# A hybrid decoder layer with 32 experts on one core: the first expert's rows by matrix products, the router in four column groups, two row stores on SyncE and the third gather moved

## The chip, the cores and the metric

One core of a Trainium2 chip runs one layer of a decoder on 512 positions, in float32. The metric is the device time of one launch in microseconds (us). A core has five engines with an instruction queue each: TensorE (PE, its weight loads shown as PEld), VectorE (DVE), ScalarE (ACT), GpSimd (POOL) and SyncE (SP). Engines wait for each other through semaphores, and 16 DMA engines move data for all queues.

## What is computed

```python
h = rmsnorm(x, g_mix); p = h @ w_in                   # q, k, v | B, C, conv input
mix = concat(rmsnorm(attention(q, k, v), g_attn_out), rmsnorm(conv, g_conv_out))
x = x + mix @ w_out
h = rmsnorm(x, g_ffn)
logits = h @ w_router + b_router                      # 32 experts
top_val, top_idx = top_k(logits, 4); gates = softmax(top_val)
# each of the 512 tokens goes to its 4 experts:
act = clamped_swiglu(rows @ w1[e] + b1[e])            # 1024 -> 2 x 1024
y = act @ w2[e] + b2[e]                               # 1024 -> 1024
x = x + sum over the 4 experts of gate * y
out = rmsnorm(x, g_final)
```

## The kernel before

**Stages.** The first 150 us compute the projections, attention and convolution. The out-projection follows in four tiles of 128 tokens (TB = 4) and two halves of the contraction. VectorE adds each tile to the residual X (residual(t, n), line 1219), ScalarE squares and sums the rows, and VectorE writes the normed rows h2 (second_norm, 1229). ScalarE's queue stores them to DRAM as h2_rows (store_h2, 1681). TensorE transposes X (turn_h2), two engines copy the transposes to xnT (turned_h2), and router(t) (782) multiplies them with the router weights in eight full products, tokens on the partitions. VectorE's select(t) (1245) picks the four best experts of each token, rank(t) (798) counts tokens per expert by a product with a triangular matrix, and place (1267) builds 0/1 matrices pick (token by slot) for experts 0 and 1 of the run.

**Rows of an expert.** An expert of the first three in order has up to 96 rows (MANY). For these a product of pick with token numbers gives the list of tokens (tok_static), POOL fetches the rows from h2_rows by an indirect DMA (fetch, 1901), TensorE transposes them (turn_lines) and ScalarE copies the result to rowsT (turned_rows, 1709). For the later experts, POOL scatters each token's entry into a list in DRAM (16 indirect DMAs, line 1929) and reads the list back into slots (six DMAs, 1937 and 1939); VectorE turns entries to token numbers (list_tokens, 1442) and POOL scales them.

**Order of the experts.** The experts 0 and 1 come first; the others are sorted by their number of rows. VectorE does the sort (1319 to 1336), TensorE three small products with its result (866 to 868) and two for the overflow table (871, 872). VectorE waits for the latter (prefix_done, 1343) ahead of pick_third and list_entries. SyncE waits for order_ready before it loads the third expert's weights.

**The expert loop.** Per expert TensorE does, by compute(i, parity) (991): first_product(i) (w1, 8 chunks of the contraction), transposes of the next expert's rows (turn_block(i + 1)), second_product(i - 1) (w2), and transposes of this expert's activations (turn_act_of(i)). The order of each engine is written out by hand, and every engine runs its instructions in that order. VectorE does clamped, product and activated for each expert (elementwise, 1447); list_tokens stands between the first expert's and the second's. POOL's move(i) (1949) scatters results, fetches rows of expert i + 2 and copies a bias selection (select, 1858) that first_product(i + 1) waits for. Weights come through a ring of 20 slots of 1 MB; a load takes two slots, and SyncE issues it when TensorE has used the old content of both (slot_used). Expert 0 fills slots 0 to 7, expert 1 slots 8 to 15, and w2 of expert 0 slots 16 to 19. The third expert's w1 goes to slots 0 to 7, w2 of the second to 8 to 11, the fourth expert's w1 to 12 to 19, and w2 of the third expert to 0 to 3 again. 18 experts are of the big kind (96 rows), 14 of the small one (64 rows).

Of the kernel before, what the change touches and what calls it, by code (L numbers as in the profile page):

```python
# [5 lines left out]
F32 = mybir.dt.float32  # L6
# [56 lines left out]
PICKED = 3  # L63
OVF_W = 4
# [18 lines left out]
def layer_kernel(nc, x, g_mix, w_in, conv_w, sinks, g_attn_out, g_conv_out, w_out,  # L83
                 g_ffn, w_router, b_router, w1, b1, w2, b2, g_final, out):
    ctx = ExitStack()
    with ctx:
# [65 lines left out]
        ones_col = sb("ones_col", [P, 1])  # L152
        upto = sb("upto", [E, E], BF16)
# [7 lines left out]
        gain_col = sb("gain_col", [P, KT])  # L161
        conv_wc = sb("conv_wc", [P, CONV_K, CT])
# [69 lines left out]
        w_out_hi = ring1_r[:, KT // 2 * SLOT:].rearrange("p (c j n) -> p c j n", c=KT, j=2)  # L232
        cur_token = slots[:, LIST_BLOCKS, 0:2, 0:1]
# [83 lines left out]
        h2_turned, h2_stored, tokens_ready = sem("h2_turned"), sem("h2_stored"), sem("tokens_ready")  # L317
        h2T_a, h2T_b = sem("h2T_a"), sem("h2T_b")
        logits_done, wrt_ready, negtop_ready, gexp_ready = sem("logits_done"), sem("wrt_ready"), sem("negtop_ready"), sem("gexp_ready")
        chosen_ready, rank_done, entries_ready = sem("chosen_ready"), sem("rank_done"), sem("entries_ready")  # L320
        pick_ready, tok_summed, sort_ready, order_done, order_ready = sem("pick_ready"), sem("tok_summed"), sem("sort_ready"), sem("order_done"), sem("order_ready")
# [52 lines left out]
        def fetches(upto):  # L374

            return 16 * sum(2 if BIG[i] and i >= STATIC else 1 for i in range(upto + 1))
# [28 lines left out]
        def _(sp):  # L405
            with nc.allow_non_contiguous_dma(reason="small parameter columns"):
# [24 lines left out]
                sp.dma_start(gain_col[:, :], g_ffn[0].rearrange("(k p) -> p k", p=P)).then_inc(small_in, 16)  # L431

# [119 lines left out]
        def _(pe):  # L552
# [224 lines left out]
            def keep_busy(count):  # L777

                for _ in range(count):
                    mm(ps[:, 3, :], ones_bf[:, :], ones_bf[:, 0:1].to_broadcast([P, 512]), start=True, stop=True)  # L780

            def router(t):

                pe.wait_ge(h2T_a, t + 1)
                pe.wait_ge(h2T_b, t + 1)
# [6 lines left out]
                logits = ps[:, LOGIT_BANKS[t % 2], 0:E]  # L792
                for k in range(KT):
                    ins = mm(logits, xnT[:, k, t * P:(t + 1) * P], w_rt[:, k, :],
                             start=(k == 0), stop=(k == KT - 1))
                ins.then_inc(logits_done, 1)

            def rank(t):
# [4 lines left out]
                if t == 2:  # L803
                    pe.wait_ge(pick_ready, 2 * t)
# [43 lines left out]
            rank(3)  # L848
            keep_busy(5)

            pe.wait_ge(pick_ready, 2 * TB)
            for e in range(2):
                for t in range(TB):
                    for part in range(2):
                        ins = mm(ps[:, 5, e:e + 1], pick[:, e, t, :], tok_value[:, t, part:part + 1],
                                 start=(t == 0 and part == 0), stop=(t == TB - 1 and part == 1))
            ins.then_inc(tok_summed, 1)

            mm(ps[0:E, 4, 0:1], chosen_cum[:, TB, :], ones_bf[:, 0:1], start=True, stop=True)
            mm(ps[0:E, 4, E:2 * E], ones_bf[:, 0:E], chosen_cum[:, TB, :], start=True, stop=True).then_inc(counts_done, 1)  # L860
# [3 lines left out]
            keep_busy(14)  # L864
            pe.wait_ge(sort_ready, 1)
            mm(ps[0:1, 5, 2 * E:3 * E], expert_no[:, :], in_place[:, :], start=True, stop=True)
            mm(ps[0:3 * E, 5, 3 * E:4 * E], ident_bf[:, :, :].rearrange("e s f -> e (s f)"), in_place[:, :], start=True, stop=True)
            mm(ps[:, 5, 4 * E:6 * E], ones_bf[0:E, :], diag[:, :, :].rearrange("e s f -> e (s f)"), start=True, stop=True).then_inc(order_done, 1)
            keep_busy(8)
            pe.wait_ge(nb_ready, 1)  # L870
            mm(ps[0:OVF_ROWS, 4, 6 * E:7 * E], ovf_nb16[:, :], upto[:, :], start=True, stop=True)
            mm(ps[0:OVF_ROWS, 4, 7 * E:8 * E], ovf_nb16[:, :], ident_bf[:, 0, :], start=True, stop=True).then_inc(prefix_done, 1)
# [44 lines left out]
            def w1_product(big, parity, slot, x_of, amid=None):  # L917

                for k0 in range(0, KT, GROUP):
                    if k0 and amid:  # L920
                        amid()
                    for k in range(k0, k0 + GROUP):
                        r, done, value = slot(k)
# [67 lines left out]
            def compute(i, parity):  # L991
# [3 lines left out]
                if i:  # L995
# [4 lines left out]
                    second_product(i - 1, 1 - parity, B_Y)  # L1000
                    turn_act_of(i)

            keep_busy(8)
            turn_block(0)
            expert_blocks(compute)
            pe.wait_ge(lin_ready, E)
# [1013 lines left out]
```

## Time and profile before

| | us |
|---|---|
| median of 3 runs | 1217.02 (1215.52 to 1218.39) |
| the profiled execution, its own time | 1214.39 |
| its span | 1212.7 |
| PE busy in the span | 1162.1 (96%) |
| DVE, ACT, POOL busy | 308.2, 190.7, 179.8 |

The page's 40 slices show the DMA engines at 9 tenths or more from the seventh slice on, at about 425 GB/s in most, and PE at 9 almost all the way. The largest groups of instructions are the experts' products (L927, L934, L953, L959). PE's durations are modelled and overlap, so two engines can both look full: the waits, and the time that a load takes to land, tell which one holds the other. Line numbers are those of the kernel before; "<-" behind a row names what ended the idle time before it.

### The profile page before, as it was taken

The page shows a single profiled execution, that of the slowest core. Times are in us where ns is not written, and L with a number is a line of the kernel's source. Part 1 is how long each engine was busy: PE and PEld are TensorE (multiplying, and loading weights), DVE is VectorE, ACT ScalarE, POOL GpSimd, SP SyncE. Part 2 cuts the span into 40 slices and gives each one's busy share as a digit, 9 for nine tenths or more (in the row PEclk, how much of TensorE's full clock was granted, in tenths as well). Part 3 has the DMA queues.
Part 4 walks back from the last instruction along what each step waited for, and adds up shares of the span by engine and source line. Part 5 has one row for each costly group of instructions (what it writes and reads, how often), then busy time and mean ns, then how long its engine had stood idle before and what let it go on. Part 6 is the DMA issues. An engine that isn't in the chain of part 4 may idle for free. (4 is left out here: it accounts for less than half of the span.)

```text
span 1212.7 us, 16574 instructions
## 1 busy us (share of the span) xinstructions
PE 1162.1 (96%) x7102; PEld 480.4 (40%) x7102; DVE 308.2 (25%) x492; ACT 190.7 (16%) x378; POOL 179.8 (15%) x251
## 2 busy tenths in 40 slices
PE   8999999999999999999999999999999999999980
PEld 5777786333333333333333333333333333333330
DVE  6588667421111111111111111111111111111117
ACT  5443612100110100001100000110000011000002
POOL 5300000521211111110111111111111101111000
PEclk9999999999999999999999999999999999999995
DMA  9602665999999999999999999999999999999996
GB/s 326 218 1 70 234 269 198 318 379 426 424 428 425 427 424 426 425 426 427 427 425 423 428 427 425 426 426 428 425 426 427 425 425 425 428 424 427 425 374 252
DMA packets 52236, 454.40 MB, mean 375 GB/s; under 512 B 13108, under 2 KB 14404, under 8 KB 27488
## 3 DMA queue, kind: packets, MB, share of 16 engines
q1 hardware_dynamic: 43760, 433.90, 86.4%
q0 software_dynamic: 7664, 17.05, 3.7%
q10 hardware_dynamic: 736, 2.36, 0.5%
q8 instruction: 58, 0.95, 0.3%
q14 instruction: 18, 0.15, 0.0%
HBM read 442.73 MB, written 15.12 MB: 378 GB/s over the span
## 5 line engine op out<-in xcount | busy, mean ns | idle before, releaser
L927 PE MATMUL ps<-ring_a,blockT 128*64 128x512 f32 x1088 | 240.6, 594 | 4.6 <-DMA ring_a<-in_w 4.6
L1416 DVE TENSOR_SCALAR glu_c<-ps 128x768 f32<-128x768 f32 (+1 forms) x32 | 26.9, 842 | 786.1 <-PE ps L934 498.0
L927 PEld LDWEIGHTS ps<-ring_a,blockT 128*64 128x64 f32 x1088 | 75.3, 137 | 159.2 <-issue 146.2
L953 PE MATMUL ps<-ring_a,actT 128*64 128x512 f32 x608 | 136.7, 596 | 0.0
L1895 POOL DMA_INDIRECT scores<-h_rows,slots x29 | 30.7, 1059 | 487.5 <-PE ps L885 486.6
L1705 ACT ACTIVATE blockT<-ps 128x512 f32<-128x512 f32 x29 | 17.3, 597 | 542.9 <-PE ps L885 542.9
L927 PE MATMUL ps<-ring_b,blockT 128*64 128x512 f32 x384 | 85.1, 594 | 2.9 <-DMA ring_b<-in_w 2.9
L1911 POOL DMA_INDIRECT expert_rows<-normed,slots x32 | 33.4, 1043 | 270.1 <-ACT normed L1734 269.8
L934 PE MATMUL ps<-ring_a,blockT 128*32 128x512 f32 x608 | 72.4, 615 | 0.0
L953 PEld LDWEIGHTS ps<-ring_a,actT 128*64 128x64 f32 x608 | 41.6, 136 | 76.2 <-issue 74.3
L927 PEld LDWEIGHTS ps<-ring_b,blockT 128*64 128x64 f32 x384 | 26.6, 137 | 57.6 <-issue 52.1
L1438 DVE TENSOR_TENSOR glu_c<-lin_c,sig 128x512 f32<-128x512 f32 (+1 forms) x50 | 43.2, 921 | 3.4 <-ACT sig L1728 2.8
L927 PE MATMUL ps<-ring_c,blockT 128*64 128x512 f32 x192 | 43.5, 595 | 0.0
L927 PE MATMUL ps<-ring_d,blockT 128*64 128x512 f32 x192 | 43.2, 592 | 0.0
L953 PE MATMUL ps<-ring_b,actT 128*64 128x512 f32 x192 | 43.0, 595 | 0.0
L959 PE MATMUL ps<-ring_a,actT 128*32 128x256 f32 x704 | 42.5, 382 | 0.0
L600 PE MATMUL ps<-xnT_hi,ring_r 128*128 128x512 f32 x144 | 36.7, 397 | 1.4 <-DVE xnT_lo L1061 1.3
L934 PEld LDWEIGHTS ps<-ring_a,blockT 128*32 128x32 f32 x608 | 17.3, 108 | 52.4 <-issue 52.4
L596 PE MATMUL ps<-xnT_hi,ring_r 128*128 128x512 f32 x144 | 35.8, 391 | 1.7 <-DVE ring_r L1054 1.7
L927 PE MATMUL ps<-ring_a,rowsT 128*64 128x512 f32 x160 | 35.2, 594 | 1.0 <-ACT rowsT L1714 1.0
L1733 ACT ACTIVATE normed<-ps,slots 128x256 f32<-128x256 f32 x18 | 8.5, 474 | 173.0 <-PE ps L959 173.0
L589 PE MATMUL ps<-xnT_lo,ring_r 128*128 128x512 f32 x144 | 35.6, 389 | 0.0
(328 smaller groups left out, 1254.9 us busy)
## 6 DMA issues: line engine op xcount, KB each, us to landing
ring_a<-in_w SPq DMA_DIRECT2D x116, 2048.0 KB, 32.2
ring_b<-in_w SPq DMA_DIRECT2D x38, 2048.0 KB, 31.0
ring_d<-in_w SPq DMA_DIRECT2D x19, 2048.0 KB, 34.6
ring_c<-in_w SPq DMA_DIRECT2D x19, 2048.0 KB
ring_a<-expert_rows SPq DMA_DIRECT2D x16, 512.0 KB, 18.4
ring<-in_w_in SPq DMA_DIRECT2D x8, 768.0 KB, 20.7
X<-in_x SPq DMA_DIRECT2D x8, 512.0 KB, 6.4
ring<-in_w_out SPq DMA_DIRECT2D x8, 512.0 KB, 5.0
```

Source lines behind the costliest of these rows:

```text
L589: ins = mm(ps[:, bank, :], high[:, k, :], xnT_lo[:, :, k, :], start=False, stop=(last and k == KT - 1))
L596: ins = mm(ps[:, bank, :], low[:, k, :], xnT_hi[:, k, :], start=False, stop=(last and k == KT - 1))
L600: mm(ps[:, bank, :], high[:, k, :], xnT_hi[:, k, :], start=(k == 0), stop=False)
L927: ins = mm(ps[half * HALF:(half + 1) * HALF, b, :], x_of(k)[0], ring(r)[:, 0, at + half * 512:at + (half + 1) * 512], start=False, stop=(k ...
L934: mm(ps[q * QUARTER:(q + 1) * QUARTER, B_BOTH, :], x_of(k)[1], quarter_cols(w, q), start=False, stop=(k == KT - 1), tile_position=(0, q * ...
L953: ins = mm(ps[half * HALF:(half + 1) * HALF, bank, :], actT[:, s % 2 * W2_K + j, s // 2 * HALF:(s // 2 + 1) * HALF], ring(r)[:, 0, j * D + ...
L959: ins = mm(ps[q * QUARTER:(q + 1) * QUARTER, bank + 1, 0:256], actT[:, 4 + j, s * QUARTER:(s + 1) * QUARTER], ring(slot(s)[0])[:, 0, j * D ...
L1416: v.tensor_scalar(width(glu_c, big), width(ps_glu, big), LIMIT, None, ALU.min).then_inc(glu_ready, 1)
L1438: ins = v.tensor_tensor(turned.rearrange("p (k q) -> p q k", k=n), a_in.rearrange("p (q k) -> p q k", k=n), b_in.rearrange("p (q k) -> p q ...
L1705: a.activation(out[:, 0:4, :], ps[:, B_T, :].rearrange("p (c t) -> p c t", c=4), ACT.Copy).then_inc(done, 1 if big else 2)
L1895: g.indirect_dma_start(gathered[:, 0:512], None, h2_halves, bass.IndirectOffsetOnAxis(lists[:, HALVES, 0:1], 0), bounds_check=last_half_to ...
L1911: g.indirect_dma_start(y_halves, bass.IndirectOffsetOnAxis(slots[:, HALVES, i, 0:1], 0), gated_y[:, parity, 0:512], None, bounds_check=las ...
```

## The change

Expert 0's rows no longer come by a gather. After place, VectorE writes for each tile of tokens a float32 matrix first_pick(t) (128 tokens by 96 slots) that holds the row's 1/rms where token and slot match; TensorE multiplies the residual X with it (pick_rows, 8 chunks for each of 4 tiles), and ScalarE copies the sums to rowsT with the norm's gain as its scale (gain_chunk, a further small load at the start). The router has the weights as stationary operand, 32 columns, and two rounds of four chunks in four column groups; ScalarE copies the partial logits, and one product with stacked identities adds them up (logits). second_norm for the tiles 2 and 3 comes after the selections, and SyncE stores these rows. SyncE's load of slot 12 no longer waits for the first gather. The third expert's gather (fetch(2)) stands ahead of the 16 list scatters in POOL's order. The small products for sort, overflow table and third list stand inside expert 0's first product (before chunks 2, 4 and 6). VectorE's selections, copies and places are in another order.

```diff
@@ SyncE
-            load_first(4, 10)
-            sp.wait_ge(rows_in, fetches(0))
-            load_first(12)
+            load_first(4, 10, 12)
             sp.wait_ge(logits_done, TB)
             load_w2(0, 0, w2_slot(0, 0))
+            for t in range(2, TB):
+                sp.wait_ge(h2_ready, 2 * (t + 1))
+                sp.dma_start(h2_tiles[t, :, :], normed[:, t % 2, :]).then_inc(h2_late, 16)
             for i in range(2, E):
                 load(i, i % 2)
@@ TensorE
             def router(t):
                 pe.wait_ge(h2T_a, t + 1)
-                pe.wait_ge(h2T_b, t + 1)
...
                 for k in range(KT):
-                    ins = mm(logits, xnT[:, k, t * P:(t + 1) * P], w_rt[:, k, :],
-                             start=(k == 0), stop=(k == KT - 1))
-                ins.then_inc(logits_done, 1)
+                    g = k % 4
+                    if k == 4:
+                        pe.wait_ge(h2T_b, t + 1)
+                    ins = mm(ps[g * E:(g + 1) * E, bank, PARTS_AT:PARTS_AT + P], w_rt[:, k, :], xnT[:, k, t * P:(t + 1) * P],
+                             start=(k < 4), stop=(k >= 4), tile_position=(0, g * E))
+                ins.then_inc(parts_done, 1)
+
+            def logits(t):
+                pe.wait_ge(parts_ready, t + 1)
+                mm(ps[:, LOGIT_BANKS[t % 2], 0:E], logit_parts, stacked[:, :], start=True, stop=True).then_inc(logits_done, 1)
...
-            out_proj(3, 1, lambda: router(1))
+            out_proj(3, 1, lambda: (logits(0), router(1)))
             turn_h2(2)
+            logits(1)
+            keep_busy(3)
+            turn_h2(3)
             rank(0)
+            keep_busy(2)
+            def pick_rows(t, chunks=range(KT)):
+                pe.wait_ge(first_pick_ready, t + 1)
+                for k in chunks:
+                    by_chunk = X[:, t, :].rearrange("p (s q j) -> p s j q", j=2, q=P)
+                    ins = mm(ps[:, PICK_BANKS[k // 4], k % 4 * MANY:(k % 4 + 1) * MANY], by_chunk[:, k // 2, k % 2, :], first_pick(t),
+                             start=(t == 0 and k % 4 == 0), stop=(t == TB - 1 and k % 4 == 3))
+                return ins
+            router(2)
             rank(1)
-            turn_h2(3)
-            router(2)
             router(3)
-            pe.wait_ge(biases_ready, 2)
-            pe.wait_ge(cur_ready, 2)
-            keep_busy(4)
+            logits(2)
+            pick_rows(0)
+            logits(3)
+            pick_rows(1, range(4))
             rank(2)
-            keep_busy(8)
+            pick_rows(1, range(4, KT))
+            keep_busy(1)
+            pick_rows(2, range(4))
             rank(3)
-            keep_busy(5)
...
+            pick_rows(2, range(4, KT))
+            pick_rows(3).then_inc(rows_turned, 1)
...
+                if i == 0:
+                    amid = {2: order_sums, GROUP: overflow_sums, GROUP + 2: third_sums}
...
-            keep_busy(8)
-            turn_block(0)
             expert_blocks(compute)
@@ VectorE
             def place(first, end):
...
                 for t in range(first, end):
-                    for e in range(2):
-                        v.tensor_scalar(pick[:, e, t, :], iota_r[:, :], own_rank[:, t, e:e + 1], None, ALU.is_equal).then_inc(pick_ready, 1)
+                    v.tensor_scalar(first_pick(t), iota_r[:, 0:MANY], own_rank[:, t, 0:1], stat[:, H_R + t:H_R + t + 1],
+                                    ALU.is_equal, ALU.mult).then_inc(first_pick_ready, 1)
...
-            second_norm(2)
+            norm_scale(2)
             select(0)
-            select(1)
             residual(3, 1)
             turned_h2(2)
+            select(1)
+            turned_h2(3)
+            norm_scale(3)
             place(0, 2)
-            turned_h2(3)
+            select(2)
+            select(3, lambda: place(2, 3))
+            place(3, 4)
+            second_picks(0, TB)
+            second_norm(2)
             second_norm(3)
-            select(2)
-            select(3)
-            place(2, 4)
@@ ScalarE
+                if isinstance(i, int) and i == 0:
+                    for k in range(KT):
+                        ins = a.activation(rowsT[:, k, :], ps[:, PICK_BANKS[k // 4], k % 4 * MANY:(k % 4 + 1) * MANY], ACT.Copy,
+                                           scale=gain_chunk[:, k:k + 1])
+                        if k % 4 == 3:
+                            ins.then_inc(rows_ready, 1)
@@ POOL
-            pool.wait_ge(h2_stored, 16 * TB)
+            pool.wait_ge(h2_stored, 16 * 2)
+            pool.wait_ge(h2_late, 16 * 2)
             pool.wait_ge(rows_cleared, 1)
             pool.wait_ge(tok_ready, 1)
-            fetch(0)
-            pool.wait_ge(rows_turned, 1)
             fetch(1)
+            pool.wait_ge(tok_ready, 2)
+            pool.wait_ge(rows_turned, 2)
+            fetch(2)
             pool.wait_ge(list_written, 16)
             pool.wait_ge(entries_ready, TB + 1)
             for t in range(TB):
...
                     g.indirect_dma_start(list_dram, bass.IndirectOffsetOnAxis(row_i[:, t, k:k + 1], 0), entry[:, t, k, :], None,
-            pool.wait_ge(tok_ready, 2)
-            pool.wait_ge(rows_turned, 2)
-            fetch(2)
             pool.wait_ge(list_written, 16 * (1 + TB * TOPK))
```

## Rows read from the trace of the kernel before

**Rows 1.** Two stretches: us, busy us by engine, granted TensorE clock, DMA share, GB/s

```profile
core 0: us, PE busy (x) PEld busy (x) DVE busy (x) ACT busy (x) POOL busy (x), PEclk, DMA share, GB/s
280.00:920.00 640.00, 640.00 (x4038) 216.48 (x4038) 81.87 (x123) 62.04 (x119) 87.27 (x90) 1.00 1.01 426
920.00:1180.00 260.00, 250.83 (x1574) 84.73 (x1568) 34.46 (x46) 25.93 (x49) 32.68 (x33) 1.00 1.00 422
```

**Rows 2.** DMA issues of 262 to 264, 276 to 277, 281 to 282: us to landing

```profile
ring_b<-in_w SPq DMA_DIRECT2D x1, 2048.0 KB, 7.7
...
ring_d<-in_w SPq DMA_DIRECT2D x1, 2048.0 KB, 10.6
...
ring_a<-in_w SPq DMA_DIRECT2D x1, 2048.0 KB, 10.9
```

**Rows 3.** SyncE in order of time: start us, us, instruction

```profile
276.58 0.33 SPq L440 DMA_DIRECT2D ring_d<-in_w  x1
281.30 3.77 SPq L445 DMA_DIRECT2D ring_a<-in_w  x2
```

**Rows 4.** TensorE in order of time: first product, next transposes, second activation's, third expert

```profile
216.58 7.09 PE L927 MATMUL ps<-ring_a,rowsT 128*64 128x512 f32 x32 [1.02 <-ACT rowsT L1714]
...
238.43 0.88 PE L878 MATMUL ps<-ident,scores 96*128 96x96 f32 x8
...
276.23 0.87 PE L885 MATMUL ps<-ident,glu_c 128*128 128x128 f32 x6
...
277.49 13.90 PE L927 MATMUL ps<-ring_a,rowsT 128*64 128x512 f32 x64
```

**Rows 5.** POOL in order of time: the first gather, the first list scatter

```profile
209.40 1.10 POOL L1904 DMA_INDIRECT scores<-h_rows,tok_static  x1 [66.83 <-DMA h_rows<-normed]
...
223.74 1.03 POOL L1929 DMA_INDIRECT slot_list<-entry,row_i  x1 [6.94 <-DVE entry L1390]
```

**Rows 6.** All engines in order of time: gain load, router, selection, residual, copy, rates

```profile
55.00 0.42 DVE L1154 TENSOR_TENSOR w_rt<-w_rt,gain_col 128x256 f32<-128x256 f32 x1 [10.24 <-DMA gain_col<-in_g_ffn]
...
189.50 1.86 PEld L794 LDWEIGHTS ps<-w_rt,xnT 128*128 128x128 f32 x16 [0.44 <-ACT xnT L1667]
189.50 1.97 PE L794 MATMUL ps<-w_rt,xnT 128*128 128x32 f32 x16
190.53 0.24 DVE L1249 SCALAR_TENSOR_TENSOR logit<-ps,stat,b_rt 128x32 f32<-128x32 f32 x1
...
192.45 0.25 DVE L1249 SCALAR_TENSOR_TENSOR logit<-ps,stat,b_rt 128x32 f32<-128x32 f32 x1
...
194.37 0.75 DVE L1225 SCALAR_TENSOR_TENSOR X<-ps,r_group,X 128x512 f32<-128x512 f32 x1
...
197.39 0.69 DVE L1242 COPY xnT<-ps 128x512 f32<-128x512 f32 x1
...
268.92 1.93 PE L959 MATMUL ps<-ring_c,actT 128*32 128x256 f32 x32
...
276.45 0.47 ACT L1733 ACTIVATE normed<-ps,slots 128x256 f32<-128x256 f32 x1 [9.96 <-PE ps L959]
```

**Rows 7.** VectorE in order of time: sort's begin and end; slot reads, clamp, activation

```profile
206.64 0.16 DVE L1310 TENSOR_SCALAR tok_static<-ps 128x2 int32<-128x2 f32 x1 [0.65 <-PE ps L855]
...
210.22 0.26 DVE L1328 TENSOR_SCALAR diag<-ident_bf,sort_f 32x32 bf16<-32x32 bf16 x1
...
263.37 0.20 DVE L1445 TENSOR_SCALAR slots<-slots 128x64 int32<-128x64 int32 x1 [19.30 <-DMA slots<-slot_list]
264.17 0.96 DVE L1416 TENSOR_SCALAR glu_c<-ps 128x768 f32<-128x768 f32 x1 [0.60 <-PE ps L934]
...
267.16 1.67 DVE L1438 TENSOR_TENSOR glu_c<-lin_c,sig 128x256 f32<-128x256 f32 x2
```

**Rows 8.** Three stretches with the granted clock (columns as in rows 1)

```profile
200.00:200.50 0.50, 0.50 (x4) 0.50 (x4) 0.44 (x4) 0.50 (x1) 0.00 (x0) 0.50 0.99 426
...
203.00:203.50 0.50, 0.50 (x3) 0.20 (x2) 0.35 (x2) 0.00 (x0) 0.00 (x0) 0.60 1.36 557
...
1186.00:1187.00 1.00, 0.00 (x0) 0.00 (x0) 0.97 (x2) 0.29 (x2) 0.51 (x1) 0.72 0.95 266
```

More of the change, by code:

```diff
@@ L63 @@
 PICKED = 3
+PICK_BANKS = (4, 3)
+COUNT_BANK = 6
+PARTS_AT = 128
 OVF_W = 4
@@ L374, in fetches @@
         def fetches(upto):
-            return 16 * sum(2 if BIG[i] and i >= STATIC else 1 for i in range(upto + 1))
+            return 16 * sum(2 if BIG[i] and i >= PICKED else 1 for i in range(1, upto + 1))
         def scatters(parity, upto):
@@ L851, in _ @@
-            pe.wait_ge(pick_ready, 2 * TB)
-            for e in range(2):
[L853 to L856, printed above, removed]
+            pick_rows(2, range(4, KT))
+            pick_rows(3).then_inc(rows_turned, 1)
+            pe.wait_ge(pick_ready, TB)
+            for t in range(TB):
+                for part in range(2):
+                    ins = mm(ps[:, 5, 1:2], pick[:, 1, t, :], tok_value[:, t, part:part + 1],
+                             start=(t == 0 and part == 0), stop=(t == TB - 1 and part == 1))
@@ L915, in turn_act_of, with w1_product @@
                 turn(act_v, BIG[i], act_turned)
-            def w1_product(big, parity, slot, x_of, amid=None):
+            def w1_product(big, parity, slot, x_of, amid={}):
                 for k0 in range(0, KT, GROUP):
-                    if k0 and amid:
-                        amid()
                     for k in range(k0, k0 + GROUP):
+                        if k in amid:
+                            amid[k]()
                         r, done, value = slot(k)
@@ L1276, in place, with second_picks @@
                 for t in range(first, end):
-                    for e in range(2):
-                        v.tensor_scalar(pick[:, e, t, :], iota_r[:, :], own_rank[:, t, e:e + 1], None, ALU.is_equal).then_inc(pick_ready, 1)
+                    v.tensor_scalar(first_pick(t), iota_r[:, 0:MANY], own_rank[:, t, 0:1], stat[:, H_R + t:H_R + t + 1],
+                                    ALU.is_equal, ALU.mult).then_inc(first_pick_ready, 1)
+            def second_picks(first, end):
+                for t in range(first, end):
+                    v.tensor_scalar(pick[:, 1, t, :], iota_r[:, :], own_rank[:, t, 1:2], None, ALU.is_equal).then_inc(pick_ready, 1)
             residual(0, 0)
@@ L1684, in store_h2, with keep_parts @@
                 act.dma_start(h2_tiles[t, :, :], normed[:, t % 2, :]).then_inc(h2_stored, 16)
+            def keep_parts(t):
+                act.wait_ge(parts_done, t + 1)
+                if t == 0:
+                    act.wait_ge(list_written, 16)
+                else:
+                    act.wait_ge(logits_done, t)
+                a.activation(logit_parts, ps[:, LOGIT_BANKS[t % 2], PARTS_AT:PARTS_AT + P], ACT.Copy).then_inc(parts_ready, 1)
             load_sqrt()
@@ L1697, in _ @@
             turned_h2(3)
-            store_h2(3)
+            keep_parts(2)
+            keep_parts(3)
             for t in range(TB):
@@ L1829, in _ @@
                 then(keep_unless_zero(expert_sel[:, :], -s * E, [[-1, E]], 1, 1.0))
+            then(g.memset(stacked[:, :], 0.0))
+            for s in range(4):
+                then(keep_unless_zero(stacked[:, :], -s * E, [[-1, E]], 1, 1.0))
             g.iota(iota_e[:, :], [[1, E]], base=0, channel_multiplier=0, allow_small_or_imprecise_dtypes=True)
```

83 lines of the change are left out of this document (52 added, 31 removed).

## The prediction

> **What bounds the kernel now.** I read the stretches first. From 280 to 920 us TensorE is never idle, and the DMA engines are full as well (share 1.01 at 426 GB/s); from 920 to 1180 TensorE loses 9.2 us while the DMA share stays at 1.00 [rows 1]. So the end is set by the weight stream, and TensorE has up to 9.2 us to give. The question is then where the stream stops being paced by TensorE, which frees the ring's slots. The landing times say it [rows 2]: the load issued at 262.5 us finds an empty queue and lands after 7.7 us; one issued at 276.58 takes 10.6, the next, at 281.30, takes 10.9 [rows 2, 3]. Hence the load of 281.30 stood 3.2 us in a queue and landed at 292.2 because the one before it landed at 287.2. From it on the stream is never dry; before it each load is issued when TensorE gives back a slot. I call it load 21. The total moves by as much as load 21's landing moves, and by nothing else that happens earlier.
>
> What sets its issue: slot 0 after the first half of the third expert's first product. That product starts at 277.49, load 21 is issued 3.81 us later [rows 3, 4]. So the quantity to forecast is this start; I call it X, and the start of the very first expert product (216.58) S [rows 4].
>
> **The change, front part: S.** Today S hangs on a gather: the POOL engine issues it at 209.40, after the last row store [rows 5], and transposes and copies follow. The change puts matrix products in its place.
> - The residual of the last tile starts at 194.37 on VectorE [rows 6]. The two routers inside the out-projection took 1.97 us each [rows 6]. They become products with 32 stationary columns, four groups side by side. Thirty-two such instructions of 256 columns took 1.93 us [rows 6]; sixteen of 128 columns are a quarter of that, 0.5, and I take 0.8 with the change of array shape (bounds 0.5 and the old 1.97). Less 1.1 each: 192.2. On the other side, the extra gain load stands last in SyncE's list of small loads; VectorE waited 10.24 us for the present last one, until 55.00 [rows 6]; an issue slot more is 0.5 us (0 to 1.5). So 192.7.
> - VectorE then: residual two times 0.75, a copy of 0.69, a selection, another copy, and an estimated 0.7 for the scale, the comparison and the first two slot matrices. A selection takes 1.92 (190.53 to 192.45) [rows 6]. Sum 5.5: the first slot matrix is there at 198.2. second_norm(2) and (3) left this path; they now follow the selections.
> - TensorE: 32 products of 128x128 stationary f32, two instructions each. The old router is the nearest row: 16 such in 1.97, 0.123 each, with weight loads busy for 1.86 of it [rows 6]. I take 0.135 (the moving side grows from 32 to 96 columns), 8.6 us, with 1.2 for two logits, two ranks and a filler between them: 208.0. VectorE's later selections run beside it; by my count each slot matrix is ready before its turn. That the product hides under the next weight load is read from the router: its weight loads fill 1.86 of the 1.97 us. The Trainium skill (TensorE: Matmul & The Clock Gate, Part 3, on what overlaps and what doesn't) has a weight load overlap a running product only where the row groups differ, which they don't here. By that rule S would be 3.9 us later (third rival), by the rows it is not.
> - ScalarE: eight copies with a scale. A copy with a scale of 128x256 took 0.47 [rows 6]; a 96-column one I estimate at 0.35, 0.25 apart when they overlap: 2.1 (1.6 to 3.0), and 0.1 to hand over. S = 210.2, that is 6.4 us earlier.
>
> Cover for what moved beside it. The order of experts (order_sums, now at the third chunk, S + 3.5 = 213.7) needs VectorE's sort. Today it runs from 206.64 to 210.5 [rows 7]; it now starts after second_norm(3), at about 209, and ends at 212.9: 0.8 us of cover, so an S under 209.4 gains nothing. The two late row stores go on SyncE's queue behind load 12 and the second-product load, some 8 MB; they land near 217 and the gather behind them near 225, while TensorE wants it at S + 22.3 = 232.5. If that cover went, each us late would be a us at the end. SyncE's waits for h2_ready (until about 209) hold back all loads from the third expert on; the first of these needs slot 0, free only after half the first product, near 220. The five further constants on POOL and the wait for the list's clearing lie in the opening stage, far ahead of use: nothing.
>
> **The change, back part: X.** This part decides. The third gather now stands ahead of the sixteen list scatters on POOL, and waits for the second expert's transposes (rows_turned 2). These come at the end of the first product: 238.43 is S + 21.85 [rows 4], and 0.5 more for the sums put into it. Behind the wait stand all sixteen scatters, the six slot reads, and the third expert's bias selection. Also VectorE stops at prefix_done until the fifth chunk (S + 11), so entries_ready, which today releases the first scatter, comes near 231; that is hidden by the POOL wait. So the scatters start at S + 21.85 + 0.5 + 0.8 (transposes) + 0.3 + 1.0 + 0.3 (gather issue, as at 209.40 with the gaps) = S + 24.8 = 235.0. Today: 223.74 [rows 5]. They start 11.3 us later although S is 6.4 earlier.
>
> From the first scatter to the slot reads on VectorE it is 263.37 − 223.74 = 39.6 us today [rows 5, 7]. VectorE runs in order, and list_tokens stands ahead of the second expert's clamp. Today the reads come at 263.37 and the clamp at 264.17, just as TensorE ends [rows 7]: no slack at all. After: reads at 274.6, clamp at 274.9, activated 4.7 us later (264.17 to 267.16 + 1.67) [rows 7], at 279.5. TensorE wants that at S + 59.65 + 0.5 = 270.4 (276.23 today) [rows 4]. It stands **9 us idle**, then transposes and begins the third expert 1.3 later [rows 4]: X = S + 70.6 = 280.8, where it was S + 60.9 = 277.5.
>
> A stall of 9 us also costs the clock. Between 1186 and 1187, with TensorE idle, the granted clock leaves the upper level; the one stretch in which the engine worked at 0.50, the 1.2 GHz level, begins at 200.0 and ends within 203.0 to 203.5 [rows 8]. Some 3.3 us at half rate are 1.6 us lost, and that I take after the stall (0 to 3). Load 21 is then issued at 280.8 + 3.8 + 1.6 = 286.2, finds an empty queue (the loads before it, 6.1 us early, are in by 281), lands after 7.7 at 293.9, against 292.2: **+1.7 us**. TensorE is then 4.9 us behind; the 9.2 of idle time [rows 1] take it up.
>
> The profiled execution took 1214.39, the median is 1217.02; 1214.39 + 1.7 = 1216.1 in its own terms, and 1217.02 + 1.7 = **1218.7** for the median. Each us of S is a us of the end.
>
> **Rivals.**
> - *The list comes back sooner.* In the new place scatters and reads meet less traffic, and the chain is 31 us instead of 39.6. For it: the part after the last scatter, about half of the chain, is waiting for DMA alone. Against it: the scatters are issued by POOL one after the other, some 1.3 us each with the gap as for the gather at 209.40 [rows 5], so 20 of the 39.6 us are its own, and the loads stand equally close there. Then VectorE is done at 271.5, TensorE waits 1 us, the clock holds, load 21 follows load 20 at 286: −6.2, **1210.8**. Chance 0.17.
> - *Slower: the clock falls in the slot products.* It fell in the same place today, behind the routers [rows 8]. Price: half rate over 3.3 us, 1.7 us of S: **1220.4**. It decides from S = 210.9 on, where the end is over 0.2% late. Chance 0.20.
> - *Slower: weight loads and products don't overlap.* A product of 96 columns would cost its weight load (1.86/16 = 0.116 [rows 6]) and, at twice 96 columns at 2.4 GHz, 0.08 more: 0.196 instead of 0.135, 64 times 0.061 = 3.9 us: **1222.6**. Against it: the router's 0.123 is hardly more than its weight load [rows 6]. Chance 0.08. (This is what the Trainium skill's rule above would do.)
> - *The change doesn't do what it says*: the chain of selections and products ends no sooner than the gather did, S = 216.6, so +8.1: **1225.1**. Chance 0.06.
>
> **How the numbers follow.** The forecast has 0.49, with its own range 1215.5 to 1221.5 (bounds of router, gain load, copies and clock). About 0.2% of the time, 2.4 us, is what a measurement of this kernel tells from no change. Faster: the first rival and 0.03 of the forecast, 0.20. Same: 0.32 of the forecast. Slower: the other rivals and 0.14 of it, 0.48. The range from 1210.5 to 1224 takes in all but the last rival and the tails.
>
> **What would show it.** Right: first expert product near 210; scatters starting near 235, later than today; a wait of VectorE for the slot reads of over 30 us; TensorE idle for about 9 us before the second expert's transposes, with a granted clock of 0.5 after it; load 21 issued near 286 into an empty queue. Wrong: third expert's product before 278, or TensorE not idle there; or loads after 286 that land later again, so that the stream was not the bound I took it for.

## The result, and the profile after

The changed kernel takes 1219.89 us (median; 1218.27 to 1221.55) beside 1216.39 (1212.83 to 1218.39) for the kernel before: a ratio of 1.0039, 95% interval 1.0027 to 1.0051. Beside three experiments it was timed again: 1.0033 (1.0021 to 1.0046). It is slower, by 3.5 us between the medians and by 4.0 to 4.7 us by the two ratios. Its profiled execution took 1218.55 us with a span of 1216.9, where the one of before had 1212.7.

The bound is the old one (in the kernel before, the page has the DMA engines at 9 tenths from the eighth slice on, 212 us, not from the seventh). Two stretches of after, columns as in [rows 1], which they answer: the DMA engines are still full, and TensorE, never idle from 280 to 920 before, now loses 0.7 us there.

```profile
core 0: us, PE busy (x) PEld busy (x) DVE busy (x) ACT busy (x) POOL busy (x), PEclk, DMA share, GB/s
280.00:920.00 640.00, 639.27 (x4012) 217.25 (x4014) 82.60 (x124) 62.87 (x121) 89.66 (x93) 1.00 1.00 420
920.00:1180.00 260.00, 253.58 (x1597) 85.05 (x1594) 34.48 (x46) 24.37 (x46) 30.82 (x31) 1.00 1.01 424
```

TensorE of after in order of time (answers [rows 4]; start us, us, operation, in brackets the idle time ahead of it and what ended it): first expert's product, second expert's transposes, the transposes of its activations, the third expert's biases and product.

```profile
207.79 3.65 PE L971 MATMUL ps<-ring_a,rowsT 128*64 128x512 f32 x16 [0.90 <-ACT rowsT L1786]
...
231.22 0.88 PE L922 MATMUL ps<-ident,scores 96*128 96x96 f32 x8 [0.84 <-DMA scores<-h_rows,tok_static]
...
280.73 1.54 PE L929 MATMUL ps<-ident,glu_c 128*128 128x128 f32 x6 [12.62 <-DVE glu_c L1499]
282.20 1.06 PE L845 MATMUL ps<-bias_split,bias_sel 96*64 96x512 bf16 x4
283.06 15.44 PE L971 MATMUL ps<-ring_a,rowsT 128*64 128x512 f32 x64
```

The front part did better than wanted: S = 207.79, 8.8 us earlier. The back part gave all of it away: X = 283.06, 5.6 us later, behind 12.62 us in which TensorE did nothing. Why it stood still is read from POOL (the two gathers, the first of sixteen scatters, the slot reads, the bias selection; answers [rows 5]) and VectorE (slot reads, clamp, activation; answers [rows 7]):

```profile
220.29 1.10 POOL L1985 DMA_INDIRECT scores<-h_rows,tok_static  x1 [77.87 <-DMA h_rows<-normed]
...
232.89 1.44 POOL L1985 DMA_INDIRECT scores<-h_rows,tok_static  x1 [11.51 <-PE ps L922]
...
234.63 1.03 POOL L2012 DMA_INDIRECT slot_list<-entry,row_i  x1 [0.30 <-issue]
...
264.38 1.16 POOL L2017 DMA_DIRECT2D slots<-slot_list  x2 [8.97 <-DMA slot_list<-entry,row_i]
...
280.14 0.57 POOL L1941 COPY bias_sel<-expert_sel 96x128 bf16<-96x128 bf16 x1
```

```profile
276.07 0.20 DVE L1506 TENSOR_SCALAR slots<-slots 128x64 int32<-128x64 int32 x1 [39.26 <-DMA slots<-slot_list]
276.18 0.95 DVE L1477 TENSOR_SCALAR glu_c<-ps 128x768 f32<-128x768 f32 x1
...
279.16 1.52 DVE L1499 TENSOR_TENSOR glu_c<-lin_c,sig 128x256 f32<-128x256 f32 x2
```

POOL waits 11.51 us for the second expert's transposes (L922) before it may gather for the third, and the scatters stand behind that. VectorE stands 39.26 us before the slot reads with the second expert's clamp behind them. The clock then falls (windows; granted clock third from the right), and the stream runs dry:

```profile
272.50:273.00 0.50, 0.00 (x0) 0.00 (x0) 0.00 (x0) 0.00 (x0) 0.00 (x0) 0.50 0.73 301
...
285.00:286.00 1.00, 1.00 (x4) 0.23 (x2) 0.00 (x0) 0.00 (x0) 0.00 (x0) 0.50 0.00 0
286.00:287.00 1.00, 1.00 (x6) 0.28 (x4) 0.00 (x0) 0.00 (x0) 0.00 (x0) 0.93 0.00 0
```

TensorE worked at half clock, 1.2 GHz, from 280.73 to about 286; the DMA engines moved nothing from 285 to 287. Load 21 (SyncE in order of time, then its time to landing; answer [rows 2, 3]) goes out at 288.40 into an empty queue and lands at 295.9, 3.7 us later than before.

```profile
288.40 0.33 SPq L462 DMA_DIRECT2D ring_a<-in_w  x1
...
ring_a<-in_w SPq DMA_DIRECT2D x1, 2048.0 KB, 7.5
```

### The profile page after: what moved, and what is told of

It reads as the page before. It is cut to its first block and busy times, and to the rows that moved or that the text cites. A ratio compares the mean times of both kernels' runs of the same rounds, so it can differ in the third digit from the quotient of the medians.

```text
span 1216.9 us, 16630 instructions
## 1 busy us (share of the span) xinstructions
PE 1157.0 (95%) x7117; PEld 479.1 (39%) x7117; DVE 308.1 (25%) x493; ACT 193.1 (16%) x388; POOL 183.0 (15%) x255
## 5 line engine op out<-in xcount | busy, mean ns | idle before, releaser
L929 PE MATMUL ps<-ident,glu_c 128*128 128x128 f32 x164 | 25.6, 289 | 12.6 <-DVE glu_c L1499 12.6
```

The lines of the kernel that those rows point to most:

```text
L929: ins = pe.transpose(ps[:, B_T + c // 4, c % 4 * P:(c % 4 + 1) * P], src[:, c * P:(c + 1) * P], ident[:, :])
```

## The experiments

Ratios are to the kernel before, timed beside it on the same chip. "The list" is the chain from the first scatter through the slot reads to VectorE. The theory: the third gather's place makes the list late, the late list stops TensorE, and load 21 comes late into a dry stream.

**One: the gather put back.** Undoes one part of the change.

```
             fetch(1)
-            pool.wait_ge(tok_ready, 2)
-            pool.wait_ge(rows_turned, 2)
-            fetch(2)
             ... sixteen scatters ...
+            pool.wait_ge(tok_ready, 2)
+            pool.wait_ge(rows_turned, 2)
+            fetch(2)
```

> The changed kernel with one part undone: the third expert's gather stands again behind the sixteen scatters of the list on GpSimd. Theory (the gather's place makes the list late: its wait for the second expert's rows on TensorE holds the scatters from 228.7, when the list's entries are ready, to 234.6, and the list then keeps TensorE waiting 12.6 us): the scatters start at about 229, right behind the entries; VectorE has the slots back at about 270.5, 5.6 us earlier than the 276.1 of the changed kernel; TensorE's wait before the second expert's transposes shrinks from 12.6 to about 7 us; the third expert's first product starts at about 277.5 where it was 283.06, and the time comes to about 1215.5, 4.4 us less than the changed kernel. The price of it: the third gather lands at about 260, and TensorE may wait up to 4 us for it before the third expert's transposes, beside the list's wait. Rival A (the wait for the overflow blocks' prefix on VectorE holds the list, not the gather): the scatters cannot start before the entries, so they gain 6 us at most; the rival says that little of it reaches the slots, time about 1219 to 1220. Rival B (the late row stores on SyncE are the loss): no gain, 1220.

Measured: 0.9977 (0.9968 to 0.9986), some 7 us less than the changed kernel, and less than the kernel before. POOL and TensorE of this kernel, in order of time:

```profile
230.10 1.04 POOL L2007 DMA_INDIRECT slot_list<-entry,row_i  x1 [8.39 <-DVE entry L1451]
...
251.16 0.99 POOL L1985 DMA_INDIRECT scores<-h_rows,tok_static  x1 [0.30 <-issue]
```

```profile
258.40 0.88 PE L922 MATMUL ps<-ident,scores 96*128 96x96 f32 x8 [2.25 <-DMA scores<-h_rows,tok_static]
...
273.88 0.88 PE L929 MATMUL ps<-ident,glu_c 128*128 128x128 f32 x6 [1.45 <-DVE glu_c L1499]
```

The scatters start as VectorE's entries are ready, and the stall shrinks to 1.45, not to the 7 expected. I had not counted that TensorE comes later itself: it waits 2.25 us for the late gather, and at a clock of 0.67 from 259 to 262 and 0.50 from 262 to 263 it needs longer for the next products. Load 21 goes out at 278.95 and finds a queue again (10.2 us to land).

**Two: the same part alone, in the kernel before.** The lines of experiment one, moved the other way.

> The kernel before with one edit alone: the third expert's gather, with its two waits, ahead of the sixteen scatters, as in the changed kernel. Theory (the gather's place delays the list whatever stands ahead of it): in the kernel before the scatters began at 223.74 and the second expert's rows are transposed at 238.4 to 240; so the scatters begin at about 241 to 242, 17 to 18 us later, the slots come back at about 281 where they came at 264, TensorE stalls 10 to 13 us before the second expert's transposes, the clock falls in it, the load that was issued at 281.30 is issued at about 295, the DMA runs dry for 6 to 9 us, and the time is about 1221 to 1225, 0.6 to 0.9% over the kernel before. Rival (the early first product is what brings the stall about, and the gather's place matters only with it): 1214 to 1217.

Measured: 1223.63 us, 1.0079 (1.0066 to 1.0092). POOL and TensorE:

```profile
239.88 0.96 POOL L1904 DMA_INDIRECT scores<-h_rows,tok_static  x1 [23.28 <-PE ps L878]
241.14 1.17 POOL L1932 DMA_INDIRECT slot_list<-entry,row_i  x1 [0.30 <-issue]
```

```profile
287.40 1.54 PE L885 MATMUL ps<-ident,glu_c 128*128 128x128 f32 x6 [11.31 <-DVE glu_c L1438]
```

As the theory has it: scatters at 241.14 (241 to 242 expected), a stall of 11.3, load 21 at 294.25. The four kernels form a square:

| | gather behind the scatters | gather ahead of them |
|---|---|---|
| all else as before | 1 | 1.0079 |
| all else as changed | 0.9977 | 1.0039, 1.0033 |

The gather's place costs 0.6 to 0.8% in either row. The rest of the change gains 0.2% in one column, about 0.4% in the other. One kernel that was timed twice came out 0.23% apart (experiment five), so the gather's part is clear of that and the 0.2% is not. "The rest" is several parts at once; only the early third load was also run by itself (experiment eight).

**Three: the list read behind the second activation.** Tests the last link, VectorE's order.

```
-                if i == 0:
+                if i == 1:
                     list_tokens()
```

> The changed kernel with one edit on VectorE: the instruction that waits for the slot list (list_tokens, 39 us of waiting in the changed kernel) stands behind the second expert's activation and no longer ahead of it. The list comes as late as before, at about 276. Theory (the list reaches TensorE on two ways, VectorE's order and GpSimd's selection of the third expert's biases, and the second stands right behind the first): the wait of 12.6 us before the second expert's transposes goes, the transposes run at about 269, and TensorE then waits about as long ahead of the third expert's biases, which need the selection that GpSimd ends at 280.7; the third expert's first product starts at about 281.7 where it was 283.06, the load into the freed buffer is issued 1 to 1.5 us earlier, time 0 to 1.5 us under the changed kernel: 1.002 to 1.004 of the kernel before. Rival (VectorE's order alone is the cause): that product starts at about 270, time 1208 to 1210, 0.995.

Measured: 1.0032 (1.0020 to 1.0043), as the theory has it. TensorE:

```profile
268.20 0.87 PE L929 MATMUL ps<-ident,glu_c 128*128 128x128 f32 x6
279.32 1.07 PE L845 MATMUL ps<-bias_split,bias_sel 96*64 96x512 bf16 x4 [10.25 <-POOL bias_sel L1941]
```

The transposes now run at 268.20, and TensorE waits 10.25 us one step further on, for the third expert's biases, whose selection on POOL stands behind the same list. Taking away one wait on a late list finds the next. Load 21 went out at 285.52, 2.9 us sooner than in the changed kernel where 1 to 1.5 had been expected; the ratio shows nothing of it.

**Four: the stall filled.** 56 unused products of ones between the second product and the transposes; run twice.

```
                     second_product(i - 1, 1 - parity, B_Y)
+                    if i == 1:
+                        for _ in range(56):
+                            mm(ps[:, 3, :], ones_bf[:, :], ones_bf[:, 0:1].to_broadcast([P, 512]), start=True, stop=True)
```

> The changed kernel with 56 products of ones (128x512, 0.213 us each at full clock by the rows of the same form, 11.9 us together) into a free bank of PSUM, on TensorE between the second product of the first expert and the transposes of the second expert's activations, where it waits 12.6 us; they compute nothing that is used. The list comes as late as before. Theory (part of the loss is the clock that falls to 0.50 at 272.7 and comes back at 286): the granted clock stays 1.00 through 268 to 290; the transposes and biases behind the wait take 1.3 instead of 2.3 us, and the third expert's 64 matmuls 13.9 instead of 15.4 us; the freed buffers come 2.5 us earlier, time about 1217.4. Rival D (the clock in this stretch costs nothing, as the loads wait for the buffers in another way): 1219.9. Rival E (the whole loss is the clock): 1214 to 1216.

> The filled stall once more (56 products of ones on TensorE between the first expert's second product and the second expert's transposes), beside the changed kernel itself, as its first run came 1.8 us shorter in the profiled execution and not shorter in the median. Theory (the half clock costs about 2.5 of the 4.2 us): the load into the freed buffer is issued 2.5 to 3 us earlier than in the changed kernel, and the time is 0.15 to 0.25% under it. Rival D (the clock costs nothing at the end): equal within 0.1%.

> The changed kernel as it is, run beside the next three, so that they are compared with it on one chip. Expected: 1.003 to 1.005 of the kernel before, as in its first run (1.0039). In its trace TensorE waits about 12.6 us before the second expert's transposes, the clock is 0.50 in most of 273 to 286, and SyncE issues the first load of the second expert's weights into a freed buffer (the load at 281.30 in the kernel before) at 287 to 289.

Measured: 1.0042 (1.0029 to 1.0056) and 1.0040 (1.0026 to 1.0053), beside 1.0033 for the changed kernel in the second timing: no gain, where 0.15 to 0.25% was expected. TensorE in the second run, and two of its windows:

```profile
268.37 12.14 PE L1052 MATMUL ps<-ones_bf 128*128 128x512 bf16 x54 [0.16 <-issue]
282.07 0.88 PE L929 MATMUL ps<-ident,glu_c 128*128 128x128 f32 x6 [1.56 <-DVE glu_c L1502]
...
283.33 13.90 PE L971 MATMUL ps<-ring_a,rowsT 128*64 128x512 f32 x64
```

```profile
272.00:280.00 8.00, 7.94 (x38) 3.59 (x37) 2.48 (x5) 1.50 (x3) 1.16 (x4) 1.00 0.83 347
...
284.00:288.00 4.00, 4.00 (x20) 1.26 (x18) 0.00 (x0) 0.00 (x0) 0.57 (x1) 1.00 0.18 70
```

The clock held, the transposes took 0.88 instead of 1.54, the product 13.90 instead of 15.44, and from these transposes to load 21 it was 5.0 and 5.1 us where the changed kernel has 7.7 and 7.1 in its two profiles. So the half clock costs load 21 2.0 to 2.7 us. (In the first run the unused products themselves ran 0.8 us past the end of the wait.) The last second product started at 1178.70 and 1180.37, also earlier than in the changed kernel (1181.56, 1182.33). But from there to the end of the span these two took 36.4 and 37.0 us, all others 35.3 to 36.1. One transfer makes the difference: the last scatter of results, which the final reads wait for. Its time to landing in the changed kernel and in the second filled run:

```profile
expert_rows<-normed,slots POOLq DMA_INDIRECT x1, 7.5
expert_rows<-normed,slots POOLq DMA_INDIRECT x1, 9.1
```

It took 8.6 and 9.1 us in the two filled runs and 7.5 to 8.4 in the twelve others; without it the stretch is 27.6 to 28.1 us in all fourteen. Why it landed late in just these two stays open, and so does whether the half clock costs the end anything: the medians show no gain.

**Five: the sums for the overflow blocks one chunk earlier, alone, and with the gather put back.**

```
-                    amid = {2: order_sums, GROUP: overflow_sums, GROUP + 2: third_sums}
+                    amid = {2: order_sums, 3: overflow_sums, GROUP + 2: third_sums}
```

> The changed kernel with the overflow blocks' two small products (overflow_sums) one chunk earlier in the first expert's product, ahead of chunk 3 in place of chunk 4. VectorE waits 6.15 us for them ahead of the third expert's picks and the list's entries. Theory (the gather's place holds the scatters): the entries are ready earlier, at about 223 to 226 instead of 228.7, but GpSimd stands in the wait for the second expert's transposes, so the scatters still start at 234.6 and the third expert's first product at 283; time 1219.9, no change (within 1.5 us). Rival A (the prefix holds the list): the slots come back 3 to 6 us earlier and the time falls by 3 to 5 us, to about 1215 to 1217.

> Both edits: the third gather behind the scatters, and the overflow blocks' products one chunk earlier. Theory: the two waits stand in line, so that only both together let the scatters start early: at about 223.5 to 225, the slots back at about 264 to 266, TensorE's wait before the second expert's transposes nearly or wholly gone, the clock held at 1.00 through 272 to 286, the third expert's first product at about 270 to 273; the loads into the freed buffers then start without a gap, time about 1208 to 1211, 9 to 12 us under the changed kernel and 5 to 8 under the kernel before. Rival A: as the run with the prefix alone, 1215 to 1217. Rival C (the next link stands right behind the list: the late gather, or the bias selection on GpSimd): the slots come back early but TensorE waits for the third expert's rows or biases, time 1213 to 1215.

> The version with both edits again (the third gather behind the scatters, the overflow blocks' products one chunk earlier), beside the one with the gather amid the scatters. Expected 0.995 to 0.997 of the kernel before, as in its first run.

Alone: 1.0023 (1.0012 to 1.0033), under the changed kernel's 1.0033 and 1.0039, but the intervals overlap. The scatters start at S + 27.0, as in the changed kernel (S + 26.8): POOL's wait holds them, not VectorE's. The list came back 3.7 us sooner against S because the scatters landed 5.4 us after the last issue and not 9.0, and that time scatters from run to run (below), so I don't put it down to the edit.

With the gather put back: 0.9961 (0.9948 to 0.9975), and in a later timing 0.9984 (0.9975 to 0.9994). Both are faster than either kernel; the second lies outside the 0.995 to 0.997 that were expected, and whether the early sums add to experiment one can't be told from these. Scatters start at 225.03 and TensorE's stall is gone, but the gather behind the sixteen scatters now comes late, by 2.1 us in the first profile and 6.46 in the second (TensorE, then POOL's slot reads of the second):

```profile
263.19 1.54 PE L922 MATMUL ps<-ident,scores 96*128 96x96 f32 x8 [6.46 <-DMA scores<-h_rows,tok_static]
...
257.49 1.15 POOL L2015 DMA_DIRECT2D slots<-slot_list  x2 [10.37 <-DMA slot_list<-entry,row_i]
```

**Six: a middle place.** The kernel of experiment five, the gather behind the twelfth scatter (`if t == 2:` inside the loop over tiles).

> The version with both edits, but the third gather behind the twelfth of the sixteen scatters, not behind the sixteenth. In that version the gather landed at 258.8, TensorE waited 2.1 us for it, and the clock was near 0.7 from 259 to 265 behind that gap. Expected: the gather is issued at about 241 and lands at about 253, ahead of TensorE's demand at 256.7; the gap and the half clock are gone, the first expert's second product ends some 3.5 us earlier; the last four scatters and the slots come 1.3 us later, at about 267. Theory (the end is now set by the stream of weights, whose engines are nearly all busy there): time within 1 us of the version with both edits. Rival (TensorE's gap is on the path): 2 to 4 us less, 0.993 to 0.9945.

Measured: 0.9992 (0.9981 to 1.0002), beside 0.9984: not faster. The gather came in time, but the list did not (POOL):

```profile
240.36 1.00 POOL L1985 DMA_INDIRECT scores<-h_rows,tok_static  x1 [0.30 <-issue]
...
259.79 1.16 POOL L2016 DMA_DIRECT2D slots<-slot_list  x2 [13.31 <-DMA slot_list<-entry,row_i]
```

The wait for the scatters to land grew to 13.31 us, and TensorE stood 7.4 us before the transposes, where I had expected the slots 1.3 us later and no stall.

**Seven: the late row stores on ScalarE.** The kernel of experiment five; SyncE's two stores are issued by ScalarE behind its copies for the first expert.

> The version with both edits (the third gather behind the scatters, the overflow blocks' products one chunk earlier; 0.9961 of the kernel before), and beside it the two late stores of rows issued by ScalarE behind its eight copies for the first expert, at about 208, where SyncE issued them behind its weight loads at 205.5 and 206.8 and they took 11 to 13 us to land. If the stores wait behind the loads of the same queue, they land by about 212 to 214, the second expert's gather is issued some 7 us earlier than 221.3, and TensorE's wait for it (part of 2.5 us for gathers) is gone. Theory (the end is set by the stream of weights, which the second expert's gather does not hold up): time within 0.1% of the version with both edits. Rival B (the late stores cost the change something): 1 to 2 us less, 0.9945 to 0.9955.

Measured: 0.9988 (0.9980 to 0.9997): no gain over the version without it (0.9961, 0.9984). The second of the two stores:

```profile
h_rows<-normed ACTq DMA_DIRECT2D x1, 512.0 KB, 12.6
```

10.6 and 12.6 us to land on ScalarE's queue, 11.1 and 12.6 on SyncE's. So it is not their place behind the loads in one queue that makes them late, as I had it; nothing is gained by moving them. The last section comes back to this.

**Eight: the third load early, alone, in the kernel before.**

```
-            load_first(4, 10)
-            sp.wait_ge(rows_in, fetches(0))
-            load_first(12)
+            load_first(4, 10, 12)
```

> The kernel before with one edit: SyncE no longer waits for the first expert's gather before the load that it issued at 213.47 into the third ring; it goes out with the two loads ahead of it, at about 193, as in the changed kernel. In the kernel before the DMA engines were busy 0.44 and 0.47 of 205 to 210 and 210 to 215; by 220 us it had moved 2.2 MB less than the changed kernel. Theory (a lead of the stream at 215 is worth something only if the buffers behind it come free earlier too, and they come free when the first expert's product runs): the engines are busy to 212, but stand idle until the loads at 225.96 instead, the first gather lands 1 to 3 us later behind the load, the first expert's product starts as much later, time the same to 3 us more, 1.000 to 1.0025. Rival (the earlier load alone is where the good of the change lies): 2 to 4 us less, 0.9965 to 0.998.

Measured: 1222.99 us, 1.0071 (1.0057 to 1.0085): far worse than the 0 to 3 us expected. TensorE:

```profile
219.97 1.54 PE L876 MATMUL ps<-ident,scores 96*128 96x96 f32 x8 [5.96 <-DMA scores<-h_rows,tok_static]
222.53 1.97 PE L925 MATMUL ps<-ring_a,rowsT 128*64 128x512 f32 x4 [1.02 <-ACT rowsT L1712]
```

The first gather took 9.9 us to land instead of 4.1, TensorE stood 5.96 us, the clock fell, and the first product began at 222.53, 6.0 us later than in [rows 4]. The wait that the change removes on SyncE had guarded the gather; in the changed kernel it can go, because the first expert's rows no longer come by one.

## Why the prediction was right, step by step

Forecast 1218.7, measured 1219.89; in profiled terms 1216.1 and 1218.55. The sign and the mechanism held, and several sizes were off in both directions. The total is closer than its parts: the change was forecast at +1.7 us and measured at +4.2 between the profiled executions (+3.5 between the medians), and 1218.7 lies within 1.2 us of 1219.89 also because the kernel before came out 0.6 us under the 1217.02 that the forecast was added to.

- **Load 21 sets the end: held.** Over the fourteen profiled executions its landing lies between 287.8 and 301.9 us, and the last second product of TensorE starts 883.5 to 885.7 us after it in every one. A spread of 14 us in the landing thus comes back at the end, to within 2.2. Within these 2.2 lies a term that I left out: where load 21 found an empty queue it is 885.5 to 885.7, where it stood in one 883.5 to 885.4 (before 884.6). From before to after that made 1.1 us beyond the landing; as the range shows, it is no constant.
- **S: too late by 2.4.** The first slot product began at 197.24, about 1.0 early, and from there to the last one it took 8.4 us (9.8 forecast). The slot products ran as counted, a little faster: 24 instructions in 3.05 us, 0.127 each against 0.135, with the weight loads beside them (PEld and PE of after):

```profile
202.61 2.90 PEld L873 LDWEIGHTS ps<-w_rt,X 128*128 128x128 f32 x24
202.63 3.05 PE L873 MATMUL ps<-w_rt,X 128*128 128x96 f32 x24
```

  So the third rival falls: the loads fill 2.90 of the 3.05 us and the products hide beside them, though all of them use every row group. The rule that the Trainium skill (TensorE: Matmul & The Clock Gate, Part 3, on what overlaps and what doesn't) gives would exclude that; the trace disagrees. The same part of the Trainium skill names a second case ahead of that rule, loads into the background weight buffer, which I had left out; whether these were such loads no run here shows. The router took 0.65 (0.8 forecast). The extra gain load cost nothing: VectorE went on at 54.94, before at 55.00 [rows 6]. The second rival falls too: the granted clock was 1.00 from 195 to 208. So does the limit that I had set, that an S under 209.4 gains nothing: the sort ended at 210.5, not 212.9, and TensorE did not wait for it.
- **From S to the scatters: too short by 2.1, yet 235.0 against 234.63.** The two errors cancel. The second expert's rows were late by 0.84 us: the row stores landed at 216.6 and 219.4 (217 forecast), and the gather behind them took 10.9 us to land, not 8. This is the cover that I said costs a us for each us late. The rest of the 2.1 is the hand-over from TensorE to POOL (0.6), the gather's issue at 1.44 instead of 1.0, and 0.24. So not each us of S was a us of the end: against experiment two, where the gather stands in the same place, S is 8.6 us earlier, the first scatter 6.5 and load 21 5.9.
- **The list: too short by 1.8** (41.4 us from the first scatter to the slot reads, 39.6 taken from before). It is no constant: the runs gave 37.6 (experiment five, early sums alone) to 46.7 (six). The first rival wanted 31; no run came near.
- **The stall: 12.6 us, forecast 9.** TensorE arrived at 268.1 (270.4 forecast) because S was early, and the list came at 276.07 (274.6). But S has no part in the stall's length: TensorE's arrival follows S, and so does the list, since it follows rows_turned 2. The 3.5 us more are the two terms above, 2.1 and 1.8, less 0.3 on VectorE and 0.2 in TensorE's arrival. By experiments one and two, S and what came with it are worth 0.2 to 0.4%, against 0.6 to 0.8% for the gather's place.
- **The half clock: at load 21 too small by 1.0.** I took 1.6; in the profiled execution it was 2.6 (7.7 us from the transposes to load 21, 5.1 with the stall filled), of which 1.0 falls on transposes and biases (2.33 us, 1.3 forecast) that I had at full clock. At the end it could not be measured.

Sum at load 21: −2.4 (S) + 2.1 (to the scatters) + 1.8 (list) − 0.3 (VectorE after the reads) + 1.0 (transposes at half clock) = +2.2: issued at 288.40, forecast 286.2. It landed 0.2 us faster than I took, so 3.7 us later than before and not 1.7; with the 1.1 of the first point the last second product came 4.8 us later. The stretch behind it was 0.6 us shorter than before (of that 0.4 by the landing of the last scatter of results), which leaves the 4.2 of the profiled execution. The fourth rival falls with S.

## What to carry over

In an in-order queue a step moved ahead must be costed by what it waits for, and by everything behind it: here one gather, moved past sixteen scatters, cost 0.6 to 0.8% with either front part. Where two engines wait for the same late list, taking one wait away finds the other; move the list. And a wait that looks idle may guard a small transfer from large ones: removing it is right only together with what it guards.

## What the hardware showed that was not expected

- **Small transfers have no time of their own.** From the end of the last scatter's issue to the slot reads it was 5.4 us (experiment five, early sums alone), 5.8 (one), 9.0 (after), 11.7 (five, gather put back, later timing) and 13.3 (six), for the same sixteen scatters. A gather of 96 rows took 4.1 us to land with the engines half empty (before, first expert), 9.9 with the third load issued ahead of it (eight), 10.9 in the changed kernel, and 17.0 in the later timing of five. These times were no terms to copy from one place to another. The queues' packets tell part of it. In the changed kernel, 250 to 255 us, SyncE's queue of loads (q1) and GpSimd's of scatters (q0; columns: packets, MB, share of the 16 engines' time) moved about as many packets, though not as many bytes:

```profile
q1 hardware_dynamic: 145, 2.11, 108.7%
q0 software_dynamic: 144, 0.01, 2.1%
```

  From 242 to 244, with few loads under way, it was 19 packets beside 186. So beside a stream of loads a small packet passed at the pace of the large ones. Which packets a given scatter stood behind on each engine is not broken down here.
- **A queue of their own did not help the stores.** By the Trainium skill (DMA: Bandwidth & Descriptors, on queues, rings and completion order) an engine takes its queues' packets in turn. The trace of experiment seven agrees (211 to 214 us, loads in q1, the two stores in q10):

```profile
q1 hardware_dynamic: 65, 1.05, 91.1%
q10 hardware_dynamic: 61, 0.25, 20.2%
```

  Nearly as many packets, but a load's are of 16 KB and a store's of 4 KB. In turn with them the stores got a fifth of the bytes, and they landed after 10.6 and 12.6 us. It was the same in the kernel before, where the stores have ScalarE's queue too: the first three, with no load under way once they moved, took 2.6 to 3.5 us, the fourth, beside loads, 9.5.
- **A gap of 2.25 us was followed by half clock.** In experiment one TensorE stood from 256.15 to 258.40 and the granted clock fell to its lower level at about 260, when TensorE was at work again, to come back in 263 to 264. In the changed kernel it kept 1.00 for over 4 us of idling and fell at about 272.5.
